# A Trainium2 encoder kernel with nine gather slots of 1 MB: four for TensorE's rows and five for VectorE's, in place of three and six

## The reference, cut to what matters

```
q = (xn @ w_query)                      # 8 heads, two halves of 128 values each
sc = q . sub_keys                       # 2 x 128 scores per head; top 16 of each half
expert = top 16 of the 16 x 16 sums     # 8 x 16 = 128 experts per token, out of 16384
act = gelu(einsum('tkd,td->tk', u[expert], xn))
out = einsum('tk,tkd->td', gate * act, v[expert])
```

## Time and profile before

| | |
|---|---|
| median of 3 runs | 3001.55 us (2995.29 to 3003.43) |
| the profiled execution's own time | 3003.72 us |
| its span | 3001.3 us |
| mean granted TensorE clock | 0.865 of full |
| busy in the span: TensorE, VectorE, ScalarE, GpSimd | 77%, 71%, 27%, 36% |
| moved by the DMAs | 1059.82 MB, mean 353 GB/s |
| u rows of tile 0, gathers issued | 256 (238 to the arena, 18 to gB) |
| one dot (L1337), mean of 418 | 2285 ns |

### The profile page before, as it was taken

How to read it: one execution, slowest core, us unless ns; L and a number is a source line. 1 busy time by engine, 2 the same in 40 slices (tenths; PEclk the granted TensorE clock), 3 DMA queues, 4 the chain that set the end, 5 groups by cost and what they waited for, 6 DMA issues and landing times.

```text
span 3001.3 us, 26287 instructions
## 1 busy us (share of the span) xinstructions
PE 2305.1 (77%) x9116; PEld 1687.3 (56%) x9116; DVE 2133.9 (71%) x3126; ACT 823.9 (27%) x2106; POOL 1081.3 (36%) x1028
## 2 busy tenths in 40 slices
PE   8999999778853342899999878788443419999996
PEld 3685545667853332666665557778432316666654
DVE  0441114799999899756666678989998997566667
ACT  1241110212229895100000021213298941000000
POOL 0000000423333333444476514323333434444765
PEclk9999999889985555999999999999755559999998
DMA  6333243999999999899999969999999998999999
GB/s 257 141 112 140 112 167 156 414 407 412 385 387 422 421 414 421 298 410 409 409 409 409 368 272 417 400 406 383 393 421 409 418 420 297 410 409 409 409 409 360
DMA packets 197170, 1059.82 MB, mean 353 GB/s; under 512 B 24112, under 2 KB 24752, under 8 KB 123824
## 3 DMA queue, kind: packets, MB, share of 16 engines
q0 software_dynamic: 147456, 805.37, 66.3%
q1 hardware_dynamic: 49584, 252.80, 21.3%
HBM read 1055.59 MB, written 2.10 MB: 352 GB/s over the span
## 4 chain that ended last, share of the span: by engine, by line
DMA 45%; PE 26%; DVE 21%; issue 3%; POOL 3%; ACT 2%; DVEq 0%; SPq 0%; ACTq 0%; POOLq 0%
DMA xnT<-pvg,idx_all 14%; DMA arena<-pu,ints 14%; DMA arena<-pvg,idx_all 12%; DVE arena L1337 10%; PE bank L1526 7%; DMA arena<-pu,idx_all 6%; DVE h L1378 3%; PE bank L1613 3%; PE bank L1816 3%; PE low L1730 2%; PE bank L1765 2%; PE bank L1823 1%; PE bank L1869 1%; POOL xnT L546 1%; PE low L1719 1%
## 5 line engine op out<-in xcount | busy, mean ns | idle before, releaser
L1337 DVE CUSTOM_DVE_ANT_0 arena<-arena,low 128x2048 f32<-128x2048 f32 x418 | 944.3, 2285 | 91.2 <-DMA arena<-pu,ints 39.7
L1890 PE MATMUL low<-arena 128*128 128x512 f32 x2048 | 902.0, 600 | 29.9 <-DMA arena<-pvd 29.5
L1890 PEld LDWEIGHTS low<-arena 128*128 128x128 f32 x2048 | 600.9, 296 | 330.9 <-DMA arena<-pvd 67.6
L530 POOL DMA_INDIRECT arena<-pu,idx_all x200 | 214.4, 1072 | 869.0 <-DVE idx_all L1306 547.8
L1378 DVE SCALAR_TENSOR_TENSOR h<-arena,cst,h 128x1024 f32<-128x1024 f32 x248 | 318.6, 1285 | 163.0 <-DMA arena<-pvg,idx_all 160.2
L1378 DVE SCALAR_TENSOR_TENSOR h<-xnT,cst,h 128x1024 f32<-128x1024 f32 x248 | 318.0, 1285 | 161.5 <-DMA xnT<-pvg,idx_all 159.1
L1869 PE MATMUL bank<-arena 128*128 128x128 f32 x768 | 194.8, 434 | 294.6 <-ACT arena L853 294.6
L546 POOL DMA_INDIRECT xnT<-pvg,idx_all x256 | 289.7, 1132 | 246.6 <-DVE h L1378 189.2
L546 POOL DMA_INDIRECT arena<-pvg,idx_all x256 | 279.3, 1091 | 237.8 <-DVE h L1378 170.6
L1869 PEld LDWEIGHTS bank<-arena 128*128 128x128 f32 x768 | 167.7, 322 | 322.6 <-ACT arena L853 321.5
L572 ACT ACTIVATE h<-low 128x512 f32<-128x512 f32 x8 | 4.3, 589 | 937.7 <-PE low L1890 937.7
(11 more groups left out here) (265 smaller groups left out, 2160.5 us busy)
## 6 DMA issues: line engine op xcount, KB each, us to landing
arena<-pvd SPq DMA_DIRECT2D x256, 512.0 KB, 6.8
arena<-w_proj SPq DMA_DIRECT2D x22, 2048.0 KB, 7.8
arena<-wq SPq DMA_DIRECT2D x16, 2048.0 KB, 11.7
arena<-w_out SPq DMA_DIRECT2D x9, 2048.0 KB, 8.0
arena<-pu,ints POOLq DMA_INDIRECT x256, 12.4
xnT<-pvg,idx_all POOLq DMA_INDIRECT x256, 13.8
arena<-pvg,idx_all POOLq DMA_INDIRECT x256, 13.8
arena<-pu,idx_all POOLq DMA_INDIRECT x238, 12.0
```

The source lines that it names most:

```text
L530: nc.gpsimd.indirect_dma_start(U[t][slot], None, pu[L], bass.IndirectOffsetOnAxis(idx_p[:, d:d + 1] if t else row(n), 0)).then_inc(u_got[t ...
L1337: vec.tensor_tensor_reduce(out=u, in0=u, in1=low[:, :] if staged else xns[0], scale=1.0, scalar=0.0, op0=ALU.mult, op1=ALU.add, accum_out= ...
L1890: ins = mm(psum[2 * t + c][:, 0:VH], W[t][:, :, n], vdense[:, n % DR, c * VH:(c + 1) * VH], start=False, stop=n == NK - 1)
```

## The change

Nine slots stay nine, and they stay in the same place. VectorE's ring gets five (UT0 = 5), the turns get four (UP = 4): three behind VectorE's ring and `gB`.

```diff
-UT0, UT1, UT2, UP = 6, 7, 6, 3
+UT0, UT1, UT2, UP = 5, 7, 6, 4
...
-        UX = ring(UT0 * D, 2) + [gB[:, :]]
+        UX = ring(UT0 * D, 3) + [gB[:, :]]
...
                     if i >= UP:
                         pool.wait_ge(s["ux_tp"], 4 * (L * NUX + i - UP + 1))
-                    elif i == 2:
+                    elif i == UP - 1:
                         pool.wait_ge(s["xn_ready"], 4 * L + 4)
```

## The result

The changed kernel takes 3016.71 us (median of 5 runs, 3014.41 to 3017.85) against 3001.01 us (5 runs, 2995.29 to 3003.43). The ratio is 1.0052, with a 95% interval of 1.0041 to 1.0063: slower by 12 to 19 us. The forecast was 3008 us, within 2993 to 3020 us. So the direction and the range held, and the loss is more than twice what the sum said, 15.7 us in place of 7.

What follows compares the result with a forecast made beforehand. Tile 1 was taken as bound by the DMAs, with VectorE and DMA limits almost coinciding in tile 0. 2.5 + 1.8 + 1.2 - 1 + 2 = +6.5 us on 3003.72, less 2.2 to the median: 3008 us, range 2993 to 3020.

Steps and rivals of the forecast that it cites:

- (b): Tile 0's long waits, 5.67 and 7.62 us, beside a weight load: +1.8 and +1.2 us, becoming about 7.5 and 9.
- (d): Ends of the runs of dots after the routing gap, about six per layer: 0.17 us each, +2 us.
- Removed, the waits for TensorE's slots: GpSimd's 70.0 us of waits per layer fall under 15; filled DMA dips are worth 1.6 and 1.9 us.
- the lag: Rows' delay before the weight load: 2.5 - 1.6 = 0.9 us in layer 0, 2.5 - 1.9 = 0.6 in layer 1.
- Added, one dot more: Every VectorE row waits one dot more, 2.2 us, or the whole routing gap; the DMAs idle 2.5 us more.
- (a): Start of layer 1, where VectorE sets the pace: one row less ahead, +2.5 us; layer 0 at 0.
- (c): Later blocks, without weight loads: small waits for rows and TensorE shrink by about half, -1 us for both layers.
- The balance: At a run's end, five rows have 15.7 us and need 15.6; before, one dot more, 2.2 us.
- Carried through tile 1: Tile 1 is bound by the DMAs, so tile 0's gain or loss goes on to the end of the layer.
- R2: Rival, chance 0.24: VectorE starves at the end of each of 12 runs, 1.5 to 2 us each: 3028 or 3018 us.
- R1: Rival, chance 0.14: the waits for TensorE were the cost and the added turn slot is enough: about 2992 us.
- R3: Rival, chance 0.22: nothing moves, each side's gain or loss is made up by the other: 3001.5 us, within 2.

Runs made afterwards that it cites:

- v5_t3: The changed kernel without its added turn slot (five VectorE slots, three turn slots, the ninth unused): 3018.51 us, ratio 1.0056.
- control: The kernel before, with tile 0's last three dots reading PSUM, so tile 1's first duplication waits for the last dot: 2996.28 us, ratio 0.9987.
- after_spread: The changed kernel with VectorE's routing spread out (pairs after k = 5, experts after k = 7, gates after k = 10): 3007.66 us, ratio 1.0029.
- before_spread: The kernel before with VectorE's routing spread out (pairs after k = 5, experts after k = 7, gates after k = 10): 3000.95 us, ratio 1.0006.

## Why the prediction was right, and where its sum was off

**Direction and range: right, and for the reason given.** The VectorE slot taken costs, the turn slot given doesn't pay for it, and the loss arises in tile 0's stretch and stays to the end of the layer. The size is off, 15.7 us in place of 7, and the terms (b) and (d) are too small.

**Removed, the waits for TensorE's slots: the mechanism held, the worth didn't.** The waits went from 70.0 to 1.6 us and their dips were filled, as written. But the sum takes 1.6 and 1.9 us of filled dips off the lag, and with the doubling in (b) that is 7 us. Without them it is 13.5 us. By v5_t3 these dips are worth 1 us with five VectorE slots, give or take 5, and the long waits don't grow where they aren't filled. Why they are worth so little wasn't tested. A reading that fits: a filled dip counts only if VectorE is later short of those very bytes, and a turn's row isn't such.

**Added, one dot more: right.** The row of the old 636.39 us went out at 644.96 us. The DMAs dipped to 242 and 139 GB/s from 644 us on and to 193 from 652, more than the 4 us at 229 that was forecast.

**(a) Start of layer 1:** +2.5 us forecast, +2.80 measured. The start of layer 0, set at 0, cost 1.24 us, inside its bounds.

**(b) The long waits: the term that was most too small.** It has 3.0 us. In the recorded pair it seems to hold in layer 0, +1.81 us from block 2 to block 4 against +1.8. That is luck: the long wait grew by 1.1 us only, from 5.67 to 6.75, and a new wait of 1.30 us at the start of block 3, which belongs to (d), makes up the rest. In layer 1 the wait fell from 7.62 to 5.68 us, and the signs "about 7.5 and 9" failed. The kernel before had these waits in its trace already, and its control didn't. Against the control the waits at block 4 grew by 6.5 and 5.2 us, or by 9.6 us in all if what the control waits more at block 5 is taken off. The short weight loads say the same by the medians: some 9 of the 15.7 us need the loads. What failed is the rule that 1 us before the load becomes 2 us after it. The control and the kernel before lie less than 1 us apart ahead of the load, and 5.5 and 7.2 us apart in the wait.

**(c) and (d), later blocks and ends of runs:** -1 and +2 us forecast for both layers, +3.79 and +3.25 us in the recorded pair from block 4 to block 8, 7.0 in place of 1. Dots at k = 1 began to wait, but by 0.2 to 2.7 us each, not by the 0.17 us of the sum. The balance behind it fails already in the kernel before. It lets the five rows start with nothing queued ahead of them, and gives the old ring a whole dot to spare. But in the kernel before the DMAs ran at 410 to 434 GB/s all through 774 to 804 us, and the very dot "wanted at 801.2 us" had to wait:

```profile
802.14 2.29 DVE L1337 CUSTOM_DVE_ANT_0 arena<-arena,low 128x2048 f32<-128x2048 f32 x1 [0.82 <-DMA arena<-pu,idx_all]
```

So the old ring was 0.8 us short there, where the sum had it 2.2 us to the good. The run after_spread, which gives 7 to 9 us back and takes most of these waits away, points to gap and run together as what the short ring can't bridge.

**Carried through tile 1:** what tile 0 lost was kept to the end of each layer, and 2.2 us were added in layer 0. Such a difference is within what traces scatter by: from the last dot of tile 0 to the first v row of layer 0 it is 358.0 us in the kernel before, 359.6 in the control, 361.3 in the changed kernel and 363.7 in before_spread.

**The rivals.** R2 is half true. The prediction calls itself wrong by a step if the new waits are above 1.5 us. Two of the eight at k = 1 of blocks 3, 5, 6 and 7 are, 2.68 and 1.65 us, and the others are 0.21 to 1.30 us. R1 is out: even with six VectorE slots kept, the fourth turn slot gives about 3 to 5 us, not 9. R3 is out.

## What to carry to other kernels

A ring must bridge the longest stretch in which its reader frees little, and then the burst that follows: count the slots against that stretch and that burst, not against mean rates. Two readers fed by one queue in order each need slots enough for their own longest pause. Beyond that a slot was worth little here (the third turn slot over 100 us, the fourth 0 to 5; the sixth VectorE slot 17 us, the seventh none). Before crediting a filled gap of the DMAs, ask who waits later for exactly those bytes. And before building a term on one long wait of one trace, look for it in a second trace with the same instructions: here it was 5.67 us in the one and 0.21 us in the other.

## What the runs showed of the hardware that was not expected

Beside a 2 MB load in another queue, a 1 MB gather that waits behind others can take much longer, and small differences go with large ones. Where the load started 7.6 us after the gather's issue, the gather took 16.80 and 19.24 us from issue to landing. Where it started 8.4 and 8.5 us after it, the gather took 11.3 and 11.59 us (the kernel before and its control, layers 0 and 1). For five slots the runs bear out the load as the cause: the waits of 3.6 to 6.8 us in three kernels were 1.2 and 1.3 us with loads of 256 KB. For six slots it fits and isn't shown apart.

Executions of the kernel before differ by up to 13 us (2993.82 to 3007.19 us in 29 runs), and the start of one dot in block 4 by 5.6 us between the kernel before and its control, with the same instructions up to there. So a single pair of traces doesn't settle terms of 2 us.
